# Decay stage of a hybrid transformer: gate rows spread by one-hot products, a low weight part made in four pieces, shorter statistics, a norm weight moved to the transposes

## The reference, cut to what matters

```python
# SSD:    y[t] = sum_s (C[t].B[s]) * exp(cs[t] - cs[s]) * dt[s] * x[s],  s <= t  (or s >= t backwards)
# mLSTM:  num[t] = sum_s (q[t].k[s]) * exp(b[t] - b[s] + ig[s] - m[t]) * v[s]
#         h[t] = num[t] / max(|den[t]|, exp(-m[t]))
```

## Time and profile before

| | |
|---|---|
| median of 3 runs | 2725.19 us (2724.61 to 2730.88) |
| the profiled execution | 2726.17 us, of which 2724.4 us are the span of its instructions |
| TensorE matmul | 2460.3 us busy, 90% of the span |
| VectorE | 1475.5 us, 54% |
| ScalarE | 1215.7 us, 45% |
| GpSimd | 595.9 us, 22% |
| decay stages | 246.97 to about 334 us, and 846.37 to about 934 us |

### The profile page before, as it was taken

How to read it: one execution, slowest core, us unless ns; L and a number is a source line. 1 busy time by engine, 2 the same in 40 slices (tenths; PEclk the granted TensorE clock), 3 DMA queues, 4 the chain that set the end, 5 groups by cost and what they waited for, 6 DMA issues and landing times. The chain is left out here.

```text
span 2724.4 us, 33139 instructions
## 1 busy us (share of the span) xinstructions
PE 2460.3 (90%) x12632; PEld 1980.2 (73%) x12632; DVE 1475.5 (54%) x2429; ACT 1215.7 (45%) x2476; POOL 595.9 (22%) x329
## 2 busy tenths in 40 slices
PE   6999887978999878959998989999999989899998
PEld 5866676757856667748786778888777767688886
DVE  1655757863855758865888433332248884333321
ACT  2446616753457517756645422222166454222221
POOL 2401305762402205742530100000025301000000
PEclk9999888998999889989998999999999989999999
DMA  4210028973200119962210122222222101122221
GB/s 139 82 47 1 16 79 319 354 267 130 68 32 1 33 76 354 357 242 78 78 63 1 70 82 93 93 93 92 68 78 80 61 1 70 64 97 98 98 85 54
DMA packets 54877, 285.56 MB, mean 105 GB/s; under 512 B 13120, under 2 KB 13120, under 8 KB 28608
## 3 DMA queue, kind: packets, MB, share of 16 engines
q1 hardware_dynamic: 45504, 266.65, 27.3%
q0 software_dynamic: 9216, 16.80, 1.6%
HBM read 275.02 MB, written 25.17 MB: 110 GB/s over the span
## 5 line engine op out<-in xcount | busy, mean ns | idle before, releaser
L206 ACT ACTIVATE weights_hi<-weights_raw 128x2048 fp32r<-128x2048 f32 (+5 forms) x132 | 236.1, 1789 | 619.1 <-PE ps L233 602.8
L220 DVE TENSOR_TENSOR weights_lo<-weights_raw,weights_hi 128x2048 fp32r<-128x2048 f32 (+3 forms) x79 | 170.6, 2160 | 542.7 <-ACT weights_hi L206 542.7
L220 POOL TENSOR_TENSOR weights_lo<-weights_raw,weights_hi 128x2048 fp32r<-128x2048 f32 (+4 forms) x53 | 239.4, 4518 | 835.0 <-issue 437.3
L231 PE MATMUL ps<-y2t_hi,weights_hi 128*128 128x512 f32 x704 | 278.8, 396 | 10.2 <-PEq L1839 10.2
L232 PE MATMUL ps<-y2t_lo,weights_hi 128*128 128x512 f32 x704 | 280.8, 399 | 0.0
L233 PE MATMUL ps<-y2t_hi,weights_lo 128*128 128x512 f32 x704 | 279.9, 398 | 0.0
L231 PE MATMUL ps<-weights_hi,attn_ht_hi 128*128 128x512 f32 (+2 forms) x576 | 205.6, 357 | 8.4 <-DVE weights_lo L220 6.9
L232 PE MATMUL ps<-weights_lo,attn_ht_hi 128*128 128x512 f32 (+2 forms) x576 | 202.2, 351 | 0.0
L233 PE MATMUL ps<-weights_hi,attn_ht_lo 128*128 128x512 f32 (+2 forms) x576 | 201.3, 349 | 0.0
L231 PEld LDWEIGHTS ps<-y2t_hi,weights_hi 128*128 128x128 f32 x704 | 133.3, 189 | 43.7 <-DVE weights_lo L220 10.7
L232 PEld LDWEIGHTS ps<-y2t_lo,weights_hi 128*128 128x128 f32 x704 | 133.3, 189 | 32.6
(11 more groups left out here) (484 smaller groups left out, 5657.2 us busy)
## 6 DMA issues: line engine op xcount, KB each, us to landing
weights_raw<-in_stream SPq DMA_DIRECT2D x106, 1024.0 KB, 4.8
weights_raw<-in_expert_gu SPq DMA_DIRECT2D x34, 1024.0 KB, 8.9
expert_raw<-in_expert_gu SPq DMA_DIRECT2D x30, 1024.0 KB, 9.1
expert_raw<-in_expert_down SPq DMA_DIRECT2D x18, 1024.0 KB, 7.7
weights_raw<-in_expert_down SPq DMA_DIRECT2D x14, 1024.0 KB, 7.7
weights_raw<-in_stream SPq DMA_DIRECT2D x12, 960.0 KB, 4.6
weights_raw<-in_stream SPq DMA_DIRECT2D x8, 700.0 KB, 8.8
weights_raw<-in_stream SPq DMA_DIRECT2D x8, 584.0 KB, 4.0
```

What stands on the lines that cost most here:

```text
L206: self.nc.scalar.activation(self.split_tiles(u)[0][:, 0:n], self.env.raw[:, u % self.RAW, 0:n], ACT.Copy).then_inc(self.hi_ready, 1)
L220: eng.tensor_tensor(lo[:, 0:n], self.env.raw[:, u % self.RAW, 0:n], hi[:, 0:n].bitcast(F32), ALU.subtract).then_inc(self.lo_ready, 1)
L231: nc.tensor.matmul(out, a[0], b[0], start=start, stop=False, **more)
```

## The change

- The gate rows of units 2 to 15 are no longer spread by four float32 products each. During unit 0 TensorE transposes the 24 gate columns of every tile into one PSUM bank (four transposes), ScalarE copies the high part, VectorE makes the low part, and from unit 2 on a row is picked and spread by two float32r matmuls of 512 columns, with a one-hot column of a 24 x 24 identity, broadcast, as the weights. `values_stage` makes that identity with one more copy.
- GpSimd makes the low part of the weight unit in four pieces of 512 columns: two before the masks of the last unit, two after.
- L1412 and L1414 become one instruction, and so do L1481 and L1482.
- The SSD norm weight is no longer multiplied in by VectorE (L1494); it becomes a per-partition scale of the transposes of the two SSD chunks. It leaves the broadcast table `vec1` (256 floats in each partition less) and is loaded by a transfer of its own.

```diff
+    def lo_part(self, eng, u, i, parts):
+        if i == 0:
+            eng.wait_ge(self.hi_ready, u + 1)
+            self.lo_split = u + 1
+        n = int(np.prod(self.sources[u].shape[1:])) // parts
+        c = slice(i * n, (i + 1) * n)
+        hi, lo = self.split_tiles(u)
+        ins = eng.tensor_tensor(lo[:, c], self.env.raw[:, u % self.RAW, c], hi[:, c].bitcast(F32), ALU.subtract)
+        if i == parts - 1:
+            ins.then_inc(self.lo_ready, 1)
...
@@ decay_stage, TensorE
-                        for t in range(T):
-                            r = cols[:, t, units[i]["row"]:units[i]["row"] + 1].to_broadcast([P, P])
-                            last = nc.tensor.matmul(ps[:, 4 + i % 2, t * P:(t + 1) * P], r, ident, start=True, stop=True)
+                        row = units[i]["row"]
+                        if i < 2:
+                            for t in range(T):
+                                r = cols[:, t, row:row + 1].to_broadcast([P, P])
+                                last = nc.tensor.matmul(ps[:, 4 + i % 2, t * P:(t + 1) * P], r, ident, start=True, stop=True)
+                        else:
+                            pe.wait_ge(rows_lo, 1)
+                            last = exact_product(nc, ps[:, 4 + i % 2, :], row_ident[:, row - FIRST:row - FIRST + 1].to_broadcast([R, P]),
+                                                 tuple(r[0:R, :] for r in rows), True, True)
                         last.then_inc(row_ready, 1)
+                        if i == 0:
+                            for t in range(T):
+                                last = nc.tensor.transpose(ps[0:R, 6, t * P:(t + 1) * P], cols[:, t, FIRST:FIRST + R], ident)
+                            last.then_inc(rows_turned, 1)
...
@@ VectorE, after the four weighted pieces of unit j
+                        if j == 0:
+                            dve.wait_ge(rows_hi, 1)
+                            nc.vector.tensor_tensor(rows[1][0:R, :], ps[0:R, 6, :], rows[0][0:R, :].bitcast(F32), ALU.subtract
+                                                    ).then_inc(rows_lo, 1)
...
@@ ScalarE, after the four Exp of unit i
+                    if i == 0:
+                        act.wait_ge(rows_turned, 1)
+                        nc.scalar.activation(rows[0][0:R, :], ps[0:R, 6, :], ACT.Copy).then_inc(rows_hi, 1)
...
@@ GpSimd
+                    if i == N - 1:
+                        env.stream.lo_part(nc.gpsimd, end.first_out, 0, 4)
+                        env.stream.lo_part(nc.gpsimd, end.first_out, 1, 4)
...
-                env.stream.split_lo(nc.gpsimd, end.first_out)
+                env.stream.lo_part(nc.gpsimd, end.first_out, 2, 4)
+                env.stream.lo_part(nc.gpsimd, end.first_out, 3, 4)
...
@@ the store of an mLSTM unit
-                link(v.tensor_scalar(tmp[:, :], den, -1.0, None, ALU.mult))
+                link(v.scalar_tensor_tensor(out=tmp[:, :], in0=den, scalar=-1.0, in1=cols[:, :, 16 + k],
+                                            op0=ALU.mult, op1=ALU.max))
                 link(v.tensor_tensor(tmp[:, :], tmp[:, :], den, ALU.max))
-                link(v.tensor_tensor(tmp[:, :], tmp[:, :], cols[:, :, 16 + k], ALU.max))
...
@@ values_stage
+            nc.vector.tensor_copy(row_ident[:, :], env.ident[0:24, 0:24])
...
@@ MixerEnd.head
-        link(v.tensor_scalar(self.mean[:, :], self.mean[:, :], 1.0 / ML_D, None, ALU.mult))
-        link(v.tensor_tensor(hv, hv, per_tile(self.mean[:, :], ML_D), ALU.subtract))
+        link(v.scalar_tensor_tensor(out=hv, in0=per_tile(self.mean[:, :], ML_D), scalar=-1.0 / ML_D, in1=hv,
+                                    op0=ALU.mult, op1=ALU.add))
...
@@ MixerEnd.vector
-        if i == self.GAIN:
-            dve.wait_ge(self.squared, T * SSD_G)
-            v.tensor_tensor(y, y, self.vec[:, V_SN:V_SN + W].unsqueeze(1).to_broadcast([P, T, W]), ALU.mult
-                            ).then_inc(self.times_gain, 1)
...
@@ first_mixers
+        for k in range(2):
+            turns[2 + k] = (*turns[2 + k][:2], env.ssd_gain[:, k:k + 1])
...
@@ first_small
+            return [(vec[:, :], at("vec1").to_broadcast([P, NV1])), (convw[:, :, :], at("conv1")),
+                    (env.ssd_gain[:, :], at("ssd_gain"))]
```

More of the change, by code:

```diff
@@ L61 @@
 F_CH = 256
-V_Q, V_KV, V_GB, V_MN, V_DTB, V_AL, V_SD, V_SN, V_RB = np.cumsum(
-    [0, Q_RANK, KV_RANK, 4 * ML_H, ML_H * ML_D, 2 * SSD_H, 2 * SSD_H, SSD_H, SSD_H * SSD_P]).tolist()
+V_Q, V_KV, V_GB, V_MN, V_DTB, V_AL, V_SD, V_RB = np.cumsum(
+    [0, Q_RANK, KV_RANK, 4 * ML_H, ML_H * ML_D, 2 * SSD_H, 2 * SSD_H, SSD_H]).tolist()
 NV1 = V_RB + NR
@@ L1270, in _, with decay_stage @@
                         nc.scalar.activation(yt[p][0], out(p), ACT.Copy).then_inc(hi_stored, 1)
-def decay_stage(env, units, cols, minus_cols, end):
+def decay_stage(env, units, cols, minus_cols, row_ident, end):
     nc, ps, ident = env.nc, env.ps, env.ident
     N = len(units)
+    FIRST, R = 8, 24
     names = ("products_ready", "row_ready", "gap_ready", "exp_done", "weighted", "masked", "out_ready",
-             "out_stored", "vector_step")
-    products_ready, row_ready, gap_ready, exp_done, weighted, masked, out_ready, out_stored, step = (
-        env.sem("decay", n) for n in names)
+             "out_stored", "rows_turned", "rows_hi", "rows_lo", "vector_step")
+    (products_ready, row_ready, gap_ready, exp_done, weighted, masked, out_ready, out_stored, rows_turned, rows_hi, rows_lo,
+     step) = (env.sem("decay", n) for n in names)
     new_group = [i == 0 or units[i]["group"] != units[i - 1]["group"] for i in range(N)]
@@ L1293, in decay_stage @@
         tmp = local.enter_context(nc.sbuf_tensor("decay_tmp", [P, T], F32, allow_name_mangling=True))
+        rows = pair_tile(nc, local, "decay_rows", S)
         end.room(local)
@@ L1428, in decay_units, with values_stage @@
     return units
-def values_stage(env, proj, vx, cols, minus_cols):
+def values_stage(env, proj, vx, cols, minus_cols, row_ident):
     nc = env.nc
@@ L1454 @@
 class MixerEnd:
-    GATE, SQUARES, GAIN = 2 * SSD_H + 1, 2 * SSD_H + 3, 2 * SSD_H + 6
+    GATE, SQUARES = 2 * SSD_H + 1, 2 * SSD_H + 3
     LAST = 2 * SSD_H + 2 * ML_H
@@ L1462, in __init__ @@
         self.first_out = first_out
-        names = ("gated", "squared", "times_gain", "variances", "roots", "inverse", "scaled")
-        (self.gated, self.squared, self.times_gain, self.variances, self.roots, self.inverse,
+        names = ("gated", "squared", "variances", "roots", "inverse", "scaled")
+        (self.gated, self.squared, self.variances, self.roots, self.inverse,
          self.scaled) = (env.sem("mixer_end", n) for n in names)
@@ L1538, in scalar @@
             head_roots(0, ML_H - 1)
-            act.wait_ge(self.times_gain, 1)
             act.wait_ge(self.inverse, 1)
@@ L2312, in first_mixers @@
             minus_cols = tile(rec, "minus_cols", T, 32)
-            values_stage(env, proj, vx, cols, minus_cols)
+            row_ident = rec.enter_context(nc.sbuf_tensor("row_ident", [24, 24], F32R, allow_name_mangling=True))
+            values_stage(env, proj, vx, cols, minus_cols, row_ident)
             h_sum, y_ssd = y[:, :, 512:768], y[:, :, 768:1024]
-            decay_stage(env, decay_units(proj, cols, dt, vx, vec, h_sum, y_ssd), cols, minus_cols,
+            decay_stage(env, decay_units(proj, cols, dt, vx, vec, h_sum, y_ssd), cols, minus_cols, row_ident,
                         MixerEnd(env, proj, vec, h_sum, y_ssd, first_out))
         yt_rec = pair_tile(nc, outer, "yt_rec", KD // 2, S, side="right")
-        transpose_stage(env, "y_t", pair_transposes(lambda t, k: y[:, t, D // 2 + k * P:D // 2 + (k + 1) * P], yt_rec),
-                        first_out)
+        turns = pair_transposes(lambda t, k: y[:, t, D // 2 + k * P:D // 2 + (k + 1) * P], yt_rec)
+        for k in range(2):
+            turns[2 + k] = (*turns[2 + k][:2], env.ssd_gain[:, k:k + 1])
+        transpose_stage(env, "y_t", turns, first_out)
         yt += chunks_of(yt_rec, KD // 2)
@@ L2930, in build @@
         convw = tile("convw", CC, CONV + 1)
-        env.lam_c = tile("lam_c", 2)
+        env.lam_c, env.ssd_gain = tile("lam_c", 2), tile("ssd_gain", SSD_H * SSD_P // P)
         env.stream = WeightStream(env, ctx)
@@ L2940, in first_small @@
             at = layer_of(dram, l)
-            return [(vec[:, :], at("vec1").to_broadcast([P, NV1])), (convw[:, :, :], at("conv1"))]
+            return [(vec[:, :], at("vec1").to_broadcast([P, NV1])), (convw[:, :, :], at("conv1")),
+                    (env.ssd_gain[:, :], at("ssd_gain"))]
         def second_small(l):
@@ L2956, in _ @@
                 sp.wait_ge(start_loaded, 32)
-                sp.wait_ge(small_loaded, 32)
+                sp.wait_ge(small_loaded, 48)
             @block.vector
@@ L3023, in packed @@
         "vec1": rows("mla_q_norm", "mla_kv_norm", "mlstm_gate_bias", "mlstm_norm", "ssd_dt_bias", "ssd_a_log",
-                     "ssd_d", "ssd_norm", "router_group_b", "router_expert_b"),
```

(2 more changed lines are left out.)

## The result

The changed kernel takes 2809.94 us (median of 4, 2806.59 to 2812.53) against 2725.18: a ratio of 1.03, 95% interval 1.0287 to 1.0313. I had forecast 2712 and given "slower" 4 in 100.

A forecast was written before the change was run, and what follows sets the result against it. TensorE bounds each decay stage up to unit 14's row, then a tail chain over VectorE, GpSimd and the last output. Two stages at -6.85 us make -13.7, with program start -13.5: 2712 us, range 2704 to 2719.

The forecast's parts named there:

- Rows: Row products of units 2 to 15: two float32r matmuls cost 0.47 us against 0.94, saving 0.47 a unit.
- the upper bound of 0.86: Row products: at worst two matmuls cost 0.43 us each, as the nearest float32 records do, saving only 0.08.
- The clock falls at the start: Rival, 4%: TensorE's wait of over a microsecond before unit 2's row halves its clock; 22 us in each stage, 2734 us.
- the forecast was 6.85: Each decay stage gets 6.85 us shorter: -3.7 - 2.9 - 0.4 + 0.15.
- not 3.7: Decay stage up to the row of unit 14: that row begins 3.7 us earlier.
- the prediction's own mark: Sign of a wrong prediction: row matmuls longer than 0.3 us from start to start.
- the start loses 1.0: Stage opening: transposes and the new low part delay the output of unit 0, 1.3 us lost (0.6 to 1.5).
- forecast 19.9: Tail: last output ready, and last store begins, 19.9 us after unit 14's row starts, against 22.77 before; 2.9 us earlier.
- the 0.4: End of the tail: the last store and head are shorter by 0.4 us.
- the 0.15: Turning: the scaled copies take longer on ScalarE and VectorE; only the last shows, 0.15 us lost.
- the +0.2 of the forecast: Program start: one more transfer is issued, with 128 KB less to move ahead of it; +0.2 us (-0.3 to +0.5).
- The chain from output to output: SSD units: output, store, weighting and mask take about 5.3 us for two units, nearly TensorE's pace; 0.2 us lost.

The follow-up runs named there:

- full-height kernel: Against the changed kernel, the one-hot row products contract over all 128 partitions instead of 24, the added 104 holding zeros; 2715.3 us, ratio 0.9957.
- one-piece kernel: Against the kernel with 128-high row products, the low part of the weight unit is made in one piece after all masks; 2716.26 us, ratio 0.9965.

## Why the prediction was wrong

**The step that failed** is one sentence under "Rows": "The contraction is over 24 rows instead of 128; no row of this trace shows such a one, and I see nothing by which it is slower or faster per column." I bounded the price of the matmul itself and not what it does to the clock of everything after it. At the full clock the 24-high row costs 283.35 - 282.70 = 0.65 us against 0.54 for the 128-high one, within the upper bound of 0.86; what the sum had at nothing is the clock: at 0.50 an output costs 2.3 us more. Full height against 24 parts the two kernels by 2809.9 - 2715.3 = 94.6 us, in the stages by 48.4 and 48.9 us.

**The rival that came nearest** was "The clock falls at the start". It had the right quantity and the right place, but it gave the wrong cause (the wait of about a microsecond) and hence the wrong length: it worked with 22 us of half clock in each stage. In the trace of the changed kernel the first stage is at 0.50 in all windows of 10 us from 290 to 370 and in nearly all of 260 to 280: some 100 of its 134 us. With full height the same wait of 1.12 us does nothing; without the wait the low rows still bring the clock down. In these runs the wait bears on when the clock falls, not on whether. Why height matters to whatever sets the clock is not shown by these runs; that it does, with the data, the columns and the number of instructions held equal, is.

**With the height repaired, the sum comes out, in part by luck.** The full-height kernel's stages are 6.8 and 7.2 us shorter than before; the forecast was 6.85. Its runs lie 14.0 us under those of the kernel before that were made beside them (2729.35), forecast 13.5. Term by term, in the first layer, against the earlier trace rows: from the first row product to the row of unit 14, 305.79 - 249.43 = 56.36 us instead of 59.62, 3.3 earlier and not 3.7. A row costs 0.54, not 0.47 (its two matmuls start 0.30 to 0.32 us apart, beyond the prediction's own mark), and the start loses 1.0, not 1.3. The tail of the full-height kernel:

```profile
312.75 4.68 PE L1347 MATMUL ps<-vx,decay_weighted 128*128 128x65 f32 x40
...
316.35 2.49 POOL L231 TENSOR_TENSOR weights_lo<-weights_raw,weights_hi 128x512 fp32r<-128x512 f32 x2 [1.51 <-ACT weights_hi L206]
...
318.80 1.87 POOL L1415 TENSOR_TENSOR decay_weighted<-decay_weighted,consts 128x128 f32<-128x128 f32 x4
...
320.63 2.85 POOL L231 TENSOR_TENSOR weights_lo<-weights_raw,weights_hi 128x512 fp32r<-128x512 f32 x2
...
320.73 4.48 PE L1347 MATMUL ps<-vx,decay_weighted 128*128 128x65 f32 x20 [3.29 <-POOL decay_weighted L1415]
...
322.73 1.58 DVE L1536 TENSOR_TENSOR y<-y,end_stat 128x768 f32<-128x768 f32 x1
...
325.25 0.16 DVE L1449 SCALAR_TENSOR_TENSOR decay_tmp<-ps,cols 128x4 f32<-128x4 f32 x1 [0.95 <-PE ps L1347]
...
329.98 3.64 PE L277 MATMUL ps<-consts,y 128*128 128x128 f32 x16 [4.77 <-PEq L1309]
```

The last store begins 19.46 us after the row of unit 14 (forecast 19.9, before 22.77) and waits for TensorE, as forecast: 3.3 us earlier, not 2.9. So the rows were put 0.4 too high and the tail 0.4 too low, and the two errors cancel. Masks end at 14.9 (14.6 to 15.2), the first two pieces take 1.25 us each and the last two 1.43 (forecast 1.1 to 1.3), the scaling of three heads waits for a piece (1.58 instead of 0.96), and the last output runs at half clock. From the last store to the turning 4.73 us instead of 5.13: the 0.4. From the turning to the end 5.49 instead of 5.34: the 0.15.

**Other points.** The start of the program: the second block's first transfer comes at 12.22 us before, 12.27 in the changed kernel and 12.49 in the full-height one, and at 12.04 to 12.61 in the others; the +0.2 of the forecast lies within this scatter. The chain from output to output did not bind (TensorE busy 46.95 of 47.00 us in the full-height kernel). In the changed kernel itself nothing of the tail's gain shows in the time, since the half clock covers it; its subtraction beside the fourth piece took 0.68 us instead of 0.43:

```profile
367.95 2.50 POOL L231 TENSOR_TENSOR weights_lo<-weights_raw,weights_hi 128x512 fp32r<-128x512 f32 x2
...
370.06 0.68 DVE L1517 SCALAR_TENSOR_TENSOR y<-end_mean,y 128x256 f32<-128x256 f32 x1
```

The Trainium skill, SBUF — State Buffer, "Who interferes with whom", says that a VectorE instruction with two SBUF inputs contends with a GpSimd one that reads SBUF; the trace of the one-piece kernel agrees (3.87 us instead of 0.43 for the fused instruction). The difference between the span of the full-height kernel and the sum of its stages (11.7 against 14.0 us) lies ahead of the first decay stage, which begins at 249.43 instead of 246.97 us; among the traces of these kernels that start varies from 246.69 to 250.26 with no change there that would explain it, and I leave it open.

## What to carry to other kernels

Where a change makes a matmul use few partitions, ask first what the granted clock does, and pad the contraction to the full height with zeros: the padding cost nothing that these traces show and was worth 94.6 us. Read the clock column beside the busy column: a TensorE busy for the whole window can be doing half the work. When a long GpSimd instruction stalls a VectorE one, cutting it and moving part of it out of the way helped by 1.1 to 1.4 us a stage; merging the stalled instruction into its neighbour moves the wait.

## What the runs showed of the hardware that I had not expected

- The height of a contraction counts for TensorE's clock, also where the added partitions hold zeros (24, 64, 128 high: 2809.9, 2735.6, 2715.3 us).
- Whether the clock stays up depends on where it was: the mLSTM units with full-height rows ran at 1.00 when they were entered at 1.00, and at 0.50 for 60 us when entered at 0.50.
- Unread matmuls in TensorE's waits kept it up: the last output 2.45 instead of 4.53 us, the turning 1.94 instead of 3.65.
- In the tail the clock fell although TensorE stood for only 1.57 us (the kernel with one piece: granted clock 1.00 up to that wait, 0.50 in the output behind it), so the 2.90 us of before were no measure of how long it may stand. The wait of 1.12 us at the opening of the full-height kernel left it at 1.00.
